# In the attentions, VectorE instead of GpSimd makes the low halves of weights, and the memory key/value matmuls come in eighths

## What is computed

```python
for i in range(DEPTH):                                   # DEPTH = 2
    mix = even_mixer(...) if i % 2 == 0 else odd_mixer(...)
    h = layer_norm(ALPHA * h + mix, ...)
    h = layer_norm(ALPHA * h + memory_attention(h, mem, wq, wkv, wo), ...)
    ffn = swiglu(...) if i % 2 == 0 else moe_swiglu(...)
    h = layer_norm(ALPHA * h + ffn, ...)

def memory_attention(x, mem, wq, wkv, wo):
    k, v = split(mem @ wkv)                              # mem is an input: needs nothing of x
    return softmax((x @ wq) @ k.T * scale) @ v @ wo
```

## Time and profile before

| what | us |
|---|---|
| median of 3 runs | 1780.56 (1780.45 to 1781.9) |
| span of the profiled execution | 1780.3 |
| TensorE busy | 1707.2 (96%) |
| VectorE busy | 1301.4 (73%) |
| ScalarE busy | 1073.5 (60%) |
| GpSimd busy | 122.8 (7%) |
| layer 0's attention (first scores to first transpose of `O`) | 72.2 to 162.4 |
| layer 1's attention | 554.9 to 637.8 |

### The profile page before, as it was taken

How to read it: one execution, slowest core, us unless ns; L and a number is a source line. 1 busy time by engine, 2 the same in 40 slices (tenths; PEclk the granted TensorE clock), 3 DMA queues, 4 the chain that set the end, 5 groups by cost and what they waited for, 6 DMA issues and landing times.

```text
span 1780.3 us, 22233 instructions
## 1 busy us (share of the span) xinstructions
PE 1707.2 (96%) x8060; PEld 1413.8 (79%) x8060; DVE 1301.4 (73%) x1107; ACT 1073.5 (60%) x953; POOL 122.8 (7%) x97
## 2 busy tenths in 40 slices
PE   7988989999999989899999999999999999999997
PEld 6777877888787777678888888888888888888885
DVE  4554746555655456569889989899899898898897
ACT  4466444434444335357777777777777777776773
POOL 2123100000103420110000000000000000000000
PEclk9988999999999999979999999999999999999999
DMA  9422625545554126079999999999999999899992
GB/s 311 163 71 95 213 71 182 182 152 195 189 172 152 55 95 213 25 245 371 374 327 363 386 316 376 340 353 370 338 364 375 332 358 383 319 370 379 319 370 98
DMA packets 231362, 461.14 MB, mean 259 GB/s; under 512 B 7264, under 2 KB 10352, under 8 KB 231312
## 3 DMA queue, kind: packets, MB, share of 16 engines
q1 hardware_dynamic: 229456, 454.06, 72.2%
q0 software_dynamic: 1856, 6.40, 1.3%
HBM read 459.39 MB, written 1.05 MB: 259 GB/s over the span
## 4 chain that ended last, share of the span: by engine, by line
PE 89%; DVE 7%; ACT 2%; issue 1%; DMA 0%; DVEq 0%; ACTq 0%
PE bank L353 26%; PE bank L355 26%; PE bank L354 26%; PE bank L707 2%; PE bank L397 2%; PE bank L765 1%; PE bank L637 1%; DVE neg_max L1481 1%; DVE w_lo L1307 1%; DVE X L1344 1%; DVE X L1353 1%; ACT w_hi L957 1%; PE bank L490 0%; DVE neg_max L1477 0%; PE bank L512 0%
## 5 line engine op out<-in xcount | busy, mean ns | idle before, releaser
L957 ACT ACTIVATE w_hi<-raw 128x2048 fp32r<-128x2048 f32 (+1 forms) x385 | 731.6, 1904 | 318.7 <-PE bank L355 314.1
L1744 DVE TENSOR_TENSOR w_lo<-raw,w_hi 128x2048 fp32r<-128x2048 f32 x285 | 648.2, 2291 | 103.5 <-ACT w_hi L957 92.7
L353 PE MATMUL bank<-w_hi,xe_hi 128*128 128x512 f32 x896 | 356.1, 397 | 0.0
L355 PE MATMUL bank<-w_hi,xe_lo 128*128 128x512 f32 x896 | 350.5, 391 | 0.0
L354 PE MATMUL bank<-w_lo,xe_hi 128*128 128x512 f32 x896 | 350.0, 391 | 0.0
L1307 DVE TENSOR_TENSOR w_lo<-raw,w_hi 128x2048 fp32r<-128x2048 f32 (+1 forms) x83 | 183.5, 2215 | 158.9 <-ACT w_hi L957 158.8
L353 PE MATMUL bank<-w_hi,xT_hi 128*128 128x512 f32 (+1 forms) x560 | 217.5, 388 | 7.6 <-DVE w_lo L1307 5.2
L354 PE MATMUL bank<-w_lo,xT_hi 128*128 128x512 f32 (+1 forms) x560 | 215.1, 384 | 0.0
L355 PE MATMUL bank<-w_hi,xT_lo 128*128 128x512 f32 (+1 forms) x560 | 214.9, 384 | 0.0
L355 PEld LDWEIGHTS bank<-w_hi,xe_lo 128*128 128x128 f32 x896 | 168.7, 188 | 36.1
L353 PEld LDWEIGHTS bank<-w_hi,xe_hi 128*128 128x128 f32 x896 | 169.0, 189 | 35.5 <-DVE w_lo L1744 2.2
(11 more groups left out here) (264 smaller groups left out, 1848.4 us busy)
## 6 DMA issues: line engine op xcount, KB each, us to landing
raw<-in_moe_w_gate_dram SPq DMA_DIRECT2D x96, 1024.0 KB, 7.2
raw<-in_moe_w_up_dram SPq DMA_DIRECT2D x96, 1024.0 KB, 7.3
raw<-in_moe_w_down_dram SPq DMA_DIRECT2D x96, 1024.0 KB, 7.3
raw<-in_mem_wkv_dram SPq DMA_DIRECT2D x16, 1024.0 KB, 5.0
raw_more<-in_moe_w_up_dram SPq DMA_DIRECT2D x16, 1024.0 KB, 7.6
raw_more<-in_moe_w_gate_dram SPq DMA_DIRECT2D x16, 1024.0 KB, 6.5
raw_more<-in_moe_w_down_dram SPq DMA_DIRECT2D x16, 1024.0 KB, 7.4
raw<-in_c_w_in_dram SPq DMA_DIRECT2D x12, 1024.0 KB, 5.1
```

Source lines behind the costliest of these rows:

```text
L353: nc.tensor.matmul(d, xh, hi[:, k, :], start=(first and k == 0), stop=False)
L355: m = nc.tensor.matmul(d, xl, hi[:, k, :], start=False, stop=(last and k == n - 1))
L957: return nc.scalar.activation(dst, src, ACT.Copy)
L1744: tt(w_lo[s][:, :], raw_exp[r][:, :], w_hi[s][:, :].bitcast(F32), ALU.subtract).then_inc(lo_made, 1)
```

## The change

The filler comes in eighths (one row k, six matmuls): in layer 0 at each of steps 0 to 7, and from step 8 on two eighths a step; in layer 1 twice at step 0, once at each of 1 to 6, twice at 7 and once at each of 8 to 13. Keys are transposed three steps after the block's last eighth and copied four after it; ScalarE's loop has one more step for that. The PSUM pair of a block is now that of its number (kv0 and its transposes on one pair, kv1 and its transposes on the other). GpSimd's 12 splits in the attentions are gone; VectorE makes each at the end of the step after the one in which ScalarE made the high half. In layer 0 these are VectorE's steps 1, 4, 8, 10, 12, 14 and 16, in layer 1 steps 1, 3, 7, 10 and 14; ScalarE's high halves of layer 0 move from steps 2 and 6 to 3 and 7, of layer 1 from 10 to 9, and the others stay.

```diff
-        KV_STEPS = [[(0, 2, 4, 6), (8, 9, 10, 11), (12, 13, 14, 15)], [(0, 2, 4, 6), (8, 10, 12, 13)]]
...
-        KT_STEP = [{ss[-1] + 2: blk for blk, ss in enumerate(st[:2])} for st in KV_STEPS]
-        KT_DONE = [{ss[-1] + 3: blk for blk, ss in enumerate(st[:2])} for st in KV_STEPS]
+        KV_PIECES = [[(s, b, k) for b, steps in enumerate(blks) for k, s in enumerate(steps)]
+                     for blks in ([(0, 1, 2, 3, 4, 5, 6, 7), (8, 8, 9, 9, 10, 10, 11, 11),
+                                   (12, 12, 13, 13, 14, 14, 15, 15)],
+                                  [(0, 0, 1, 2, 3, 4, 5, 6), (7, 7, 8, 9, 10, 11, 12, 13)])]
+        KV_LAST = [{b: s for s, b, _ in pieces} for pieces in KV_PIECES]
+        KV_DONE = [{s + 1: b for b, s in last.items()} for last in KV_LAST]
+        KT_STEP = [{s + 3: b for b, s in last.items() if b < 2} for last in KV_LAST]
+        KT_DONE = [{s + 4: b for b, s in last.items() if b < 2} for last in KV_LAST]
...
-        BY_POOL = set(BEHIND) | POOL_SPLIT[0] | POOL_SPLIT[1]
+        BY_POOL = set(BEHIND)
...
+                    for s, blk, k in KV_PIECES[l]:
+                        if s != i:
+                            continue
+                        name = f"{l}kv{blk}"
+                        if k == 0:
+                            p = (kv_pair + blk) % 2
+                            fill_outs[blk] = [(t, claim(pe, f"{name}.{t}", 2 * p + t, signal=False))
+                                              for t in range(TB)]
+                        c = k // CK
+                        chunk_product(blocks[name][0] + c, fill_outs[blk], mT_hi, mT_lo, CK * c,
+                                      c == 0, c == 1, W, rows=(k % CK,),
+                                      done=chunk_used if k % CK == CK - 1 else None, ready="m")
...
@@ -902,8 +905,6 @@
-            for c in sorted(POOL_SPLIT[0]):
-                split(c)
...
-                if i - 2 in KV_SPLIT[1]:
-                    split(blocks["1kv0"][0] + KV_SPLIT[1][i - 2])
...
@@ -1117,11 +1116,11 @@
-                for i in range(NU + 1):
+                for i in range(NU + 2):
...
@@ -1561,6 +1560,8 @@
                         outputs((i - 2) // 4)
+                    if i - 1 in KV_SPLIT[l]:
+                        split(blocks[f"{l}kv0"][0] + KV_SPLIT[l][i - 1])
```

More of the change, by code:

```diff
@@ L307, in trunk @@
         NU = 16
-        KV_STEPS = [[(0, 2, 4, 6), (8, 9, 10, 11), (12, 13, 14, 15)], [(0, 2, 4, 6), (8, 10, 12, 13)]]
-        KV_HALF = [{s: (blk, i) for blk, ss in enumerate(st) for i, s in enumerate(ss)}
-                   for st in KV_STEPS]
-        KV_DONE = [{ss[-1] + 1: blk for blk, ss in enumerate(st)} for st in KV_STEPS]
-        KT_STEP = [{ss[-1] + 2: blk for blk, ss in enumerate(st[:2])} for st in KV_STEPS]
-        KT_DONE = [{ss[-1] + 3: blk for blk, ss in enumerate(st[:2])} for st in KV_STEPS]
+        KV_PIECES = [[(s, b, k) for b, steps in enumerate(blks) for k, s in enumerate(steps)]
[6 more added lines that the diff above has]
+        KT_DONE = [{s + 4: b for b, s in last.items() if b < 2} for last in KV_LAST]
         KV_SPLIT = [{0: 2} | {s: 3 + n for n, s in enumerate(
-            s for ss in st for s in ss[1::2])} for st in KV_STEPS]
-        POOL_SPLIT = [{blocks[f"{l}kv0"][0] + n for n in KV_SPLIT[l].values()} for l in range(2)]
+            s for s, _, k in pieces if k % CK == CK - 1)} for pieces in KV_PIECES]
         BEHIND = [blocks[name][0] + 2 for name in ("0out1", "0mw1")]\
@@ L536, in values @@
                                      stop=True, skip_group_check=True).then_inc(sem(f"unit_done{l}"), 1)
-                fill_outs = [None]
-                def mem_kv(i, l=l, fill_outs=fill_outs):
-                    if i not in KV_HALF[l]:
-                        return
-                    blk, half = KV_HALF[l][i]
-                    name = f"{l}kv{blk}"
-                    if half == 0:
-                        p = pair[0] % 2
-                        pair[0] += 1
-                        fill_outs[0] = [(t, claim(pe, f"{name}.{t}", 2 * p + t, signal=False))
-                                        for t in range(TB)]
-                    c = half // 2
-                    chunk_product(blocks[name][0] + c, fill_outs[0], mT_hi, mT_lo, 4 * c,
-                                  c == 0, c == 1, W, rows=((0, 1), (2, 3))[half % 2],
-                                  done=chunk_used if half % 2 else None, ready="m")
@@ L558, in mem_kT @@
+                def mem_kT(i, l=l, kv_pair=kv_pair):
                     if i not in KT_STEP[l]:
                         return
-                    name = f"{l}kv{KT_STEP[l][i]}"
+                    blk = KT_STEP[l][i]
+                    name = f"{l}kv{blk}"
                     for t in range(TB):
                         wait_emptied(pe, f"{name}.{t}")
-                    transposes(f"{name}T", m_stage, 4, 2 * (pair[0] % 2))
-                    pair[0] += 1
+                    transposes(f"{name}T", m_stage, 4, 2 * ((kv_pair + blk) % 2))
```

7 lines of the change are left out of this document (5 added, 2 removed).

## The result

The changed kernel takes 1762.72 us, median of 4 runs (1762.58 to 1763.92), against 1781.23 for the kernel before on the same chip: ratio 0.9899, 95% interval 0.9885 to 0.9913. That is 18.5 us faster; 15.1 were predicted, and the time lies in the predicted range (1759 to 1772). The profiled execution took 1762.58 us; its span is 1760.6, 19.7 less than the span of before.

A forecast was written before the change was run, and what follows sets the result against it. TensorE, busy nearly throughout, was taken to bound the kernel, so only its waits and slow-clock time could be won. Layer 0's 8.8 plus layer 1's 6.3 us give 15.1 off 1780.3; with 0.3 for the median, 1765.5 us, range 1759 to 1772.

The forecast's parts named there:

- Units 0 to 7 of layer 0: Start of layer 0's attention: first scores to unit 8's scores take 25.5 us instead of 31.14, with the split covered.
- Unit 8: Layer 0: scores to Ln take 4.1 us instead of 8.43; Ln at 101.8 instead of 111.80, 10.0 us won.
- Units 8 to 15: Second half of layer 0's attention: the Ln-to-Ln chain, with uncovered splits, takes 43.5 us against 42.95, 0.6 lost.
- Behind unit 15: End of layer 0's attention, Ln to transposes of `O`, 7.7 us before: a key block copy falls into step 15, 0.6 lost.
- Layer 1: Layer 1's attention, bound by TensorE: 3.3 + 0.7 + 1.5 + 1.4 - 0.6 = 6.3 us won.
- The first wait: Layer 1: TensorE's wait of 3.30 us before the first key transposes goes, 3.3 us won.
- the slow stretch: Layer 1: the 3.4 us at 0.55 of full clock behind the first wait goes, 1.5 us won.
- The short waits: Layer 1: two short TensorE waits, 0.34 us before the transposes at 566.89 and a like one at unit 3, go; 0.7 won.
- GpSimd's gate columns: GpSimd's gate columns beside VectorE's splits: delayed up to 2.2 us, costed at nothing, at most 1 us.
- Rival A: Both attentions: place of splits does not matter, leaving about 7 us of gain, 1773; chance 0.12.
- Rival B: Layer 0, units 8 to 15: looser chain, TensorE's 5.3 us a step binds, 38.7 rather than 43.5, 1760.7; chance 0.10.
- Rival C: Layer 0, units 9 to 15: brief idling drops TensorE's clock to 1.2 GHz; five slow steps give 1787; chance 0.05.

The follow-up runs named there:

- fill_late: The changed kernel with its filler in eighths and later key transposes, but GpSimd makes the 12 splits again; 1764.26 us, ratio 0.9914.
- early_split: The changed kernel with VectorE's split directly behind the clamp and evacuations of the step, instead of at its end, except the last; 1758.36 us, ratio 0.9872.
- split_only: The changed kernel with splits still on VectorE, but filler in the old parts of 12 matmuls and key transposes nearly as before; 1764.76 us, ratio 0.9913.
- neg_on_act: fill_late with ScalarE instead of VectorE making `neg_max` in layer 1; 1760.65 us, ratio 0.9881.
- tail_split: early_split with VectorE's last split of layer 1 in step 15, behind unit 15's maximum, instead of step 14; 1754.23 us, ratio 0.9849.
- tail_again: tail_split measured once more, code unchanged; 1754.98 us, ratio 0.9851.
- keep_warm: tail_split plus thrown-away matmuls in the waits at the end of both attentions (6, 3, 6 in layer 0; 2, 5 in layer 1); 1753.02 us, ratio 0.9839.
- warm_after: The changed kernel plus thrown-away matmuls at the end of both attentions (14, 3, 6 in layer 0; 6, 5 in layer 1); 1763.97 us, ratio 0.9895.

## Why the prediction was right, point by point

- **Units 0 to 7 of layer 0.** Predicted 25.5 us to the scores of unit 8, measured 25.51; steps of 3.4, measured 3.38. Right in size, and the split there is covered (two fall into these steps, where the prediction counts three). Its steps are steps at full clock, so the sum holds a gain that it doesn't name: before, the steps 2 to 4 took 7.36, 2.91 and 6.90 us, where steps 6 and 7, with a part of the filler and without, took 4.75 and 1.94. These three steps took 5.7 us more than such steps at full clock: 2.3 are the wait at 83.56 and 3.3 the clock behind it. The splits need not leave GpSimd for most of this: in fill_late the same way takes 26.2 us.
- **Unit 8.** Predicted 4.1 us from scores to Ln, measured 101.66 - 97.51 = 4.15. The Ln came at 101.66, predicted 101.8.
- **Units 8 to 15.** Predicted 43.5 us, measured 43.56; 6.3 in a step with a split (6.35 and 6.36), 5.9 in one with a high half (5.88 and 5.89), 6.5 in the one that also copies (6.37). The clamp waits for the split, as the changed kernel's timelines show, and early_split takes that wait away. The two chains are nearly equal for another reason than "6.1 us each": before, the seven steps took 7.58, 7.19, 4.94, 5.89, 5.71, 5.89 and 5.75 us. The first two stood behind the wait of 5.47 us, at low clock (0.69 from 109.80 to 115.00), and that they are gone pays for what the split adds to the steps with it, 6.36 us against 5.75 in fill_late. The bank wait of block 2 was 1.44 (bound 1.5) and hidden.
- **Behind unit 15.** Predicted 7.7 + 0.6 = 8.3 us, measured 153.40 - 145.22 = 8.18. Layer 0: 8.8 predicted, 8.8 measured.
- **Layer 1** is the term that was mis-sized: 6.3 predicted, 9.0 measured. The first wait (3.3) and the slow stretch (1.5) went as predicted. The short waits were worth 1.2, not 0.7: before, unit 8's scores came 33.8 us after the first with 8 eighths done; now it is 35.4 with 10, and 35.4 - 2 x 1.43 = 32.6. At the end I put a new wait of 1.9, and it is 1.53 (1.8 won, not 1.4). Of the "-0.6" for more bursts little is there: an eighth costs 4.30 - 2.87 = 1.43 us in these steps, and a whole part 2.80 in split_only's (5.67 - 2.87), so a burst costs some 0.03 us and not 0.1. And I gave a price to the slow stretch behind the first wait but none to the same stretch behind the second, where before the clock was 0.59 over 4.1 us; the rest of the nine, 9.0 - 3.3 - 1.2 - 1.5 - 1.8 = 1.2 us, is that one. The traces agree: 4.1 x 0.41 = 1.7 us of that stretch went, and 3.3 x 0.14 = 0.5 came behind the new wait (0.86 from 615.51 to 618.81). It was in sight: the second wait was named, and what had been said of the first held for it too.
- **Outside the attentions** I predicted nothing. Single stages moved by up to 1.9 us: the one behind layer 1 is 1.2 longer, most likely by the clock (0.50 over the 6 us from 618, and 1.2 us more to the memory attention's transposes, 85.7 against 84.6), and the expert stage's 1.9 lies within what it varies by between kernels that do not touch it (1016.9 to 1020.1). None of it is shown to be an effect of the change. The profiled execution's 19.7 us are the 15.1 forecast, 2.7 more in layer 1, and 1.9 outside.
- **No load came late, and GpSimd's gate columns** took 671 ns on average before and after: both costed at nothing, and both nothing.
- **Rival A** (place does not matter; the evenly spread filler is what helps) had the wrong mechanism and a right half. The filler alone, with late transposes, does nearly what the whole change does (fill_late), although 27.2 us of stalls stay. My argument treated the stall's place in the chain as decisive; what decided in units 0 to 7 of layer 0 was whether enough lay between a unit's scores and its transposes, and there either cure is enough. In layer 1 it isn't so: the filler with late transposes wins 3.8 us there and the engine 8.9. The forecast was right for both parts together; it could not tell which of them did what.
- **Rival B** (TensorE's 5.3 us a step binds) was right in its price and wrong in its condition: it needs another place for the split. Then 7 steps with two transposes take 38.0, where I had 38.7.
- **Rival C** (the clock falls within units 9 to 15; its "3.5 slow steps" is 15.1 / 4.4 = 3.4) did not occur: 1.00 from 97.5 to 147. TensorE's waits came in one piece at unit 15 (4.55 us, 3 to 5 predicted), and the low clock after it.

Which instructions GpSimd's split holds up is shown by fill_late and neg_on_act: `neg_max` (1233 ns against 169) and the multiply `P` (1347 against 558), both with all operands in SBUF; not the two reductions of `S` (409 and 286 ns beside GpSimd's splits, the same without), nor the add and the clamp that read a bank. The Trainium skill, "SBUF — State Buffer", Who interferes with whom, says that on this chip reductions never contend, that an operation on two SBUF tensors contends with GpSimd's reads, and that tensor-by-scalar operations can contend when their operands meet certain conditions. The trace agrees for the reductions and for `P`, and shows both cases of the last: `neg_max`, on two values a partition, was held up, and the norm's `var_eps`, on one value (155 ns at 464.64 in the kernel before, beside a split from 461.01 to 465.62), was not.

## What to carry to other kernels

When a tiny instruction shows a mean many times its own length, look for what another engine runs beside it; then compare three cures by their price: move the large work, move the tiny instruction (3.3 us of ScalarE here did in one layer what 11.4 us of VectorE did), or put independent work between producer and consumer. They can replace each other, wholly or, as in layer 1 here, in part, so try each alone before adding up their gains. And a long instruction moved into a loop costs by its place in the step: behind the last instruction of the chain it cost 5.6 us, under another engine's turn nothing that shows, as TensorE then bound.

A wait costs its length and then the slow stretch behind it; when waits are priced, every one of them gets both terms.

## What the runs showed of the hardware that I had not expected

With the same three waits ahead of them (1.54, 0.88 and 1.67 us), the sixteen transposes of `O` ran at full clock in tail_split (1.94 us) and, with 1.54, 0.88 and 1.22, at half in tail_again (3.65 us). early_split had tail_split's very waits (1.54, 0.87 and 1.68) and 3.65 us. So a short idle time decides the clock of what follows sometimes one way and sometimes the other; thrown-away matmuls in the waits gave 1.94 us in both layers of keep_warm and of warm_after. And the clock at the start of the expert stage lost 8.5 us of TensorE's time in one execution of a kernel and 5.2 in another, with 2.5 us between the two stages; with the stages ahead of it this made one kernel's spans 4.7 us different.

In the kernel before and in fill_late, each `neg_max` that GpSimd's split held up ended with the split, within 0.04 us: it took up to 4.39 us instead of 0.23 in layer 0, and up to 3.85 instead of 0.17 in layer 1.
